# A fused decoder layer on one core: attention outputs issued for four steps at a time, with six buffers of turned probabilities and an earlier copy of one pattern's turned values

## What is computed

```python
ATTN_PATTERNS = ((128, 1), (512, 4), (2048, 16))      # window, dilation; 8 slots of 64 in each
scores = jnp.einsum("brnqhd,brnkhd->brnhqk", qb, kb) * (ATTN_HEAD_DIM ** -0.5)
scores = jnp.where(valid[None, None, :, None], scores, -jnp.inf)
m = jnp.max(scores, axis=-1, keepdims=True)
p = jnp.exp(scores - m)
den = jnp.sum(p, axis=-1)
o = jnp.einsum("brnhqk,brnkhd->brnqhd", p, vb) / jnp.moveaxis(den, -1, -2)[..., None]
lse = jnp.moveaxis(m[..., 0] + jnp.log(den), -1, -2)
```

## Time and profile before

| | |
|---|---|
| median of three runs | 2852.78 us (2850.05 to 2854.59) |
| the profiled execution | 2852.36 us, of which the span of its instructions is 2850.7 us |
| TensorE's mean granted clock | 0.987 |
| TensorE busy | 2760.1 us (97% of the span) |
| VectorE, ScalarE, GpSimd busy | 55%, 43%, 55% |
| attention block | from about 1975 to 2281 us |
| matmuls of the scores in it (L1658) | 768 |
| transposes of probabilities (L1669) | 600 |
| output products (L87 into a_pso) | 2400 |

### The profile page before, as it was taken

The page is one execution under the profiler, slowest core; times in us unless marked ns, Lnnn a source line. Parts: engine busy times, 40 slices in busy tenths (PEclk is TensorE's granted clock), DMA queues, the critical chain, the costliest instruction groups (busy, mean ns, idle before and its releaser), DMA issues. The chain is left out here.

```text
span 2850.7 us, 44158 instructions
## 1 busy us (share of the span) xinstructions
PE 2760.1 (97%) x15998; PEld 2295.0 (81%) x15998; DVE 1581.4 (55%) x2527; ACT 1238.0 (43%) x2258; POOL 1576.6 (55%) x1078
## 2 busy tenths in 40 slices
PE   6999999999999999999998999999999889999998
PEld 5888888888887888888887788887988777778787
DVE  6335334897544346885424555555777686743433
ACT  5232234333224533332234565565777654532332
POOL 7677778877777788777773454553111254322000
PEclk8999999999999999999999999999999999999999
DMA  3556345433225345332135454555665478855543
GB/s 125 142 171 216 132 133 154 129 117 96 69 72 192 118 150 148 112 110 74 60 119 185 150 187 149 191 171 168 188 204 177 126 247 257 297 186 171 170 148 110
DMA packets 462813, 436.24 MB, mean 153 GB/s; under 512 B 60736, under 2 KB 403008, under 8 KB 454976
## 3 DMA queue, kind: packets, MB, share of 16 engines
q1 hardware_dynamic: 460352, 425.79, 47.7%
q0 software_dynamic: 2304, 8.39, 0.8%
HBM read 290.99 MB, written 143.13 MB: 152 GB/s over the span
## 5 line engine op out<-in xcount | busy, mean ns | idle before, releaser
L550 PE MATMUL p_acc<-h_kept,w_hi 128*128 128x512 f32 x1216 | 475.4, 391 | 4.6 <-ACT work L596 3.1
L552 PE MATMUL p_acc<-h_kept,w_lo 128*128 128x512 f32 x1216 | 474.1, 390 | 0.0
L551 PE MATMUL p_acc<-h_kept,w_hi 128*128 128x512 f32 x1216 | 474.1, 390 | 0.0
L431 POOL TENSOR_TENSOR w_lo<-p_sums,w_hi 128x512 fp32r<-128x512 f32 x300 | 390.8, 1319 | 131.4 <-ACT w_hi L637 131.4
L637 ACT ACTIVATE w_hi<-p_sums 128x512 fp32r<-128x512 f32 x300 | 189.0, 632 | 471.8 <-PE p_acc L552 449.0
L550 PEld LDWEIGHTS p_acc<-h_kept,w_hi 128*128 128x128 f32 x1216 | 228.8, 188 | 53.9 <-ACT work L596 3.3
L552 PEld LDWEIGHTS p_acc<-h_kept,w_lo 128*128 128x128 f32 x1216 | 228.8, 188 | 47.6
L551 PEld LDWEIGHTS p_acc<-h_kept,w_hi 128*128 128x128 f32 x1216 | 228.9, 188 | 47.1
L550 PE MATMUL p_acc<-p_ops,w_hi 128*128 128x512 f32 x608 | 238.0, 391 | 7.1 <-DVE p_ops L738 7.1
L551 PE MATMUL p_acc<-p_ops,w_hi 128*128 128x512 f32 x608 | 237.3, 390 | 0.0
L552 PE MATMUL p_acc<-p_ops,w_lo 128*128 128x512 f32 x608 | 237.1, 390 | 0.0
(11 more groups left out here) (344 smaller groups left out, 6725.2 us busy)
## 6 DMA issues: line engine op xcount, KB each, us to landing
raw<-w_in SPq DMA_DIRECT2D x100, 512.0 KB, 4.7
s_qs<-p_stage SPq DMA_DIRECT2D x96, 256.0 KB, 3.9
work<-s_gates SPq DMA_DIRECT2D x48, 512.0 KB, 7.3
p_rawb<-w_in SPq DMA_DIRECT2D x38, 512.0 KB, 3.7
keep<-w_in SPq DMA_DIRECT2D x38, 512.0 KB, 4.8
s_xbc<-p_stage SPq DMA_DIRECT2D x32, 512.0 KB, 2.6
work<-s_xbc SPq DMA_DIRECT2D x16, 1024.0 KB, 6.4
spare<-s_qs SPq DMA_DIRECT2D x16, 1024.0 KB, 5.7
```

What stands on the lines that cost most here:

```text
L431: tt(w_lo[:, k], weight(u, k), w_hi[:, k], ALU.subtract).then_inc(w_made, 1)
L550: pe.matmul(bank, hi, ops[k][:, 0, c], start=c == 0, stop=False)
L551: pe.matmul(bank, hi, ops[k][:, 1, c], start=False, stop=False)
L552: last = pe.matmul(bank, lo, ops[k][:, 0, c], start=False, stop=c == 3)
```

## The change

TensorE does the outputs of four steps in every fourth step instead of those of two in every second; the turned probabilities get six buffers instead of four; VectorE copies the two groups of such a visit in the second and the third step after it instead of one in each even step; and the copies of pattern two's turned values wait for output 48i - 9, the last that reads the old ones, instead of output 48i - 4.

```diff
-        probs_t = s.sb("a_probst", [P, 4, 4, P])
+        probs_t = s.sb("a_probst", [P, 6, 4, P])
...
         def evacuate(eng, parity, copy, j):
 
             eng.wait_ge(p_turned, j + 5)
-            eng.wait_ge(o_made, j + 1)
+            eng.wait_ge(o_made, max(j - 1, 1))
...
-                copy(probs_t[:, j % 4], ps_t[:, n % 4]).then_inc(t_taken[parity], 1)
+                copy(probs_t[:, j % 6], ps_t[:, n % 4]).then_inc(t_taken[parity], 1)
...
             if pair:
-                eng.wait_ge(o_made, NS * (pair - (g == 0)) + {0: 4 * SPAN + 4, 1: 1, 2: 4}[g])
+                eng.wait_ge(o_made, NS * (pair - (g == 0)) + {0: 4 * SPAN + 4, 1: -4, 2: 4}[g])
...
-                    if j >= 4 and j % 2:
-                        output(j - 5)
-                        output(j - 4)
+                    if j >= 4 and j % 4 == 3:
+                        for n in range(j - 7, j - 3):
+                            output(n)
...
-                for j in range(ALL + 5):
+                for j in range(ALL + 7):
...
-                    if j >= 6 and j % 2 == 0:
-                        grp = j // 2 - 3
+                    if j >= 9 and j % 4 in (1, 2):
+                        grp = (j - 9) // 4 * 2 + (j % 4 == 2)
```

More of the change, by code:

```diff
@@ L1481, in evacuate @@
             if width(g, b) == width(g, b + 1) == 2 * P:
-                copy(probs_t[:, j % 4], ps_t[:, n % 4]).then_inc(t_taken[parity], 1)
+                copy(probs_t[:, j % 6], ps_t[:, n % 4]).then_inc(t_taken[parity], 1)
             elif width(g, b + 1) == P:
-                copy(probs_t[:, j % 4, 1::2], ps_t[:, n % 4, 1::2]).then_inc(t_taken[parity], 1)
+                copy(probs_t[:, j % 6, 1::2], ps_t[:, n % 4, 1::2]).then_inc(t_taken[parity], 1)
             else:
-                copy(probs_t[:, j % 4, 1:], ps_t[:, n % 4, 1:]).then_inc(t_taken[parity], 1)
+                copy(probs_t[:, j % 6, 1:], ps_t[:, n % 4, 1:]).then_inc(t_taken[parity], 1)
         def evacuate_v(eng, parity, copy, which):
@@ L1685, in output @@
                         for h in range(first, 2):
-                            last = matmul_by_columns(pe, ps_o[:, j // 2 % 2, (b + e) % 4, :OUT_W], probs_t[:, j % 4, 2 * e + h],
+                            last = matmul_by_columns(pe, ps_o[:, j // 2 % 2, (b + e) % 4, :OUT_W], probs_t[:, j % 6, 2 * e + h],
                                                      v_tok[:, g, b + e - 1 + h, sl * OUT_W:(sl + 1) * OUT_W],
```

## The result

The changed kernel takes 2861.86 us (median of 20 runs), the kernel before 2853.48 us (20 runs beside it); the ratio is 1.0029, with a 95% interval of 1.0021 to 1.0038. It is slower, by 8.4 us where 7.5 were forecast. The profiled execution took 2861.93 us, 9.6 more than that of before.

What follows compares the result with a forecast made beforehand. TensorE was taken to set the attention stage's pace. Terms -16.1 - 3.4 + 11.7 + 5.0 + 7.2 + 1.5 + 1.6 gave +7.5, so 2860.4 us, range 2850 to 2868.

Steps and rivals of the forecast that it cites:

- visits, 46 x 0.35: TensorE going to the outputs and back costs 0.35 us; 46 fewer visits up to step 188: 16.1 us less.
- waits that go: Pattern two's value copy (3 x 0.8) and transposes waiting in steps 84 to 87 (3 x 0.35): 3.4 us less.
- new waits, 18 wide stretches: Without a visit between, transposes wait for exponentials in four-step wide stretches: 0.65 us each, 11.7 us more.
- new waits, 15 narrow ones: Pattern three's stretches with narrow pieces: 0.33 us each, the middle between 0 and 0.7, 5.0 us more.
- keys, longer waits of TensorE: Second head's key load, queued behind pattern three's store, comes later; wait grows 2.4 in each of three pairs: 7.2 us.
- lower clock behind them: TensorE's clock falls behind the first pair's key wait too: 1.6 us more, between 0 and 4.8.
- tail: Copy of group 91 moves from step 188 to 190, delaying SyncE's queue at the attention stage's end: 1.5 us more.
- The walk: Step-by-step timing of a wide four-step stretch: transposes late by 0.22 and 0.35, with restarts 0.7 us together.
- Only the visits count: Rival: bursts don't wait, the chain being short enough or queues far enough ahead; 2843.7 us, chance 0.12.
- Keys in time: Rival: the key load lands earlier, so neither the 7.2 nor the clock is paid; 2851.6 us, chance 0.12.
- A lower clock in the bursts: Rival: the clock falls in a third of the 18 wide stretches, 9.6 us more; 2870 us, chance 0.06.
- The earlier copy brings nothing: Rival: another wait ends last at pattern two's values, so 2.4 us more; 2862.8 us, chance 0.05.

Runs made afterwards that it cites:

- run 3: Kernel before with one step's outputs in every step, so twice as many visits: ratio 1.0047 to the kernel before.
- run 8: Kernel before with six buffers of turned probabilities alone: ratio 0.9998 to the kernel before.
- run 7: Kernel before with only pattern two's turned values copied on their last reader: 2849.52 us, ratio 0.9984.
- runs 1 and 2: Keys of head two loaded before pattern two's store, in the changed kernel (0.9969, 2844.8 us) and in the kernel before (0.9963, 2843.78 us).
- run 9: Changed kernel with the next block's loads before the store of pattern two in the last pair: ratio 1.0005 to the kernel before.
- run 6: Changed kernel with early keys, transposes three steps after the scores and visits one step later: ratio 1.0006 to the kernel before.
- run 4: Changed kernel with each group of outputs copied one step earlier: ratio 1.0055 to the kernel before.
- run 5: Changed kernel with transposes three steps after the scores instead of two, turned-tile copies moved along: ratio 1.0054 to the kernel before.

## Why the prediction was right, step by step

From the first score to that of step 188 the changed kernel takes 8.92 us more; the stretches, each difference with 0.35 us for the visit that it no longer has, split that up. What TensorE waited behind the key splits, and what the clock took there, are worked out below.

| step of the prediction | forecast | measured |
|---|---|---|
| visits, 46 x 0.35 | -16.1 | -16.1 by a price of 0.35: 0.35 in run 3, 0.34 in steps 8 to 11 of the changed kernel |
| waits that go | -3.4 | about -2.9 |
| new waits, 18 wide stretches | +11.7 | +11.9 |
| new waits, 15 narrow ones | +5.0 | +5.2 |
| keys, longer waits of TensorE | +7.2 | +7.5 |
| lower clock behind them | +1.6 | +3.0 |
| steps 0 to 3 of pair zero, without a visit | 0 | +0.3 |
| tail | +1.5 | +1.9 |

The measured terms add up to the 10.85 us by which the block grew, 3.35 more than the forecast. The profiled executions are 9.6 apart, as the first score came 2.2 earlier and what follows the block took 1.0 longer; the medians are 8.4 apart, with an interval of the ratio that reaches from 6.0 to 10.8 us. So the mechanism and the signs were right and most terms too, but that the time came within 1 us of the forecast is partly luck.

The walk gave a loss of 0.22, 0.35 and two restarts of 0.06 in a wide stretch, and 0.26, 0.32 and the same restarts came. The middle value taken for narrow stretches was a guess between two bounds, and that it fell so well is luck: 0.27 and 0.42 in the two halves of pattern three, 0.35 on average.

*Waits that go.* The 0.8 us for the copy of pattern two's values was 0.61, in the changed kernel and alone (run 7). The sum for steps 96 to 99 left out small gaps behind value transposes. The 0.35 of steps 84 to 87 came as forecast, but neither by the six buffers (run 8) nor by the earlier values (run 7): it takes the new order of visits, and why is not shown.

*Keys.* TensorE's three waits behind the key splits were 1.56 and 2.03 and 2.24 us, and are 4.50, 4.41 and 4.41:

```profile
2222.55 0.66 PE L1669 MATMUL a_pst<-ident,a_probs 128*128 128x128 f32 x4 [2.24 <-ACT a_probs L1720]
```

```profile
2073.97 1.12 PE L1669 MATMUL a_pst<-ident,a_probs 128*128 128x128 f32 x4 [4.50 <-ACT a_probs L1720]
...
2150.99 1.12 PE L1669 MATMUL a_pst<-ident,a_probs 128*128 128x128 f32 x4 [4.41 <-ACT a_probs L1720]
...
2227.23 1.12 PE L1669 MATMUL a_pst<-ident,a_probs 128*128 128x128 f32 x4 [4.41 <-ACT a_probs L1720]
```

They grew by 2.9, 2.4 and 2.2, together 7.5 where 3 x 2.4 were forecast. At the second of them the copy, SyncE's issue of the keys right behind the store, and the split are:

```profile
2135.53 0.42 DVE L1776 COPY att_all<-a_pso 128x260 f32<-128x260 f32 x1
```

```profile
2136.59 3.44 SPq L977 DMA_DIRECT2D work<-s_kv  x2
```

```profile
2147.86 1.91 ACT L1507 ACTIVATE key_hi<-work 128x2048 fp32r<-128x2048 f32 x1 [5.02 <-DMA work<-s_kv]
```

With step 96 at 2124.70, the copy came at 10.8 (10.7 forecast, 9.5 before), and the keys 12.3 behind it (12.2 before). ScalarE stood ready at 18.1, where it was 19.8, so its own wait grew by 3.05. TensorE's grew by less, 2.4, as forecast. What the late loads cost is shown by runs 1 and 2.

*Clock.* This term was too small: 1.6 forecast, 3.0 measured, as what the waits leave of the 10.5 us in the three stretches. The windows of 6 us from the end of each wait say the same. Before, the granted clock is 1.00 behind the first, and behind the second (and, with the same 0.72, the third)

```profile
2147.23:2153.23 6.00, 6.00 (x76) 5.36 (x76) 2.23 (x10) 3.99 (x10) 6.00 (x4) 0.72 0.24 67
```

and in the changed kernel

```profile
2073.97:2079.97 6.00, 6.00 (x67) 5.67 (x69) 2.23 (x10) 4.59 (x11) 6.00 (x4) 0.59 0.26 81
2150.99:2156.99 6.00, 6.00 (x79) 5.76 (x80) 2.14 (x10) 4.59 (x11) 6.00 (x4) 0.75 0.33 101
2227.23:2233.23 6.00, 6.00 (x61) 5.67 (x63) 2.23 (x10) 4.58 (x11) 3.40 (x1) 0.56 0.21 60
```

By these windows 0.28 x 6 us are lost twice before, 3.4 in all, and now 0.41, 0.25 and 0.44 x 6 us, 6.6 in all: 3.2 more. The prediction counted one more fall, in pair one, at the size of the old ones; the falls in pairs one and three are also longer. It reads a mean clock of 0.60 as half of the time at the lower level, too: between 1.00 and 0.50 a mean of 0.60 is four fifths of the time. The 1.6 us are not touched by that.

*Tail.* One more step than before to the copy and the queue behind it; run 9 shows the queue, and that 6 us could be taken out of it.

*The rule on PSUM.* By amount VectorE and ScalarE had time to spare, and I let the walk decide against that. The Trainium skill (TensorEngine Tiling (Array Packing), Performance Considerations) says that the copies out of PSUM may become the bottleneck. The runs show a middle course: VectorE's masks and copies, which all read PSUM, do limit TensorE, but in the burst alone, where they are 1.2 us a step against 0.92 (run 6), and by the order in which they come (run 4).

*The rivals.* Only the visits count: out, the waits are there. Keys in time: out, they came later still. A lower clock in the bursts: no, between the key waits it is 1.00 (2080 to 2150 and 2155 to 2225 us of the changed kernel), with the waits of 0.3 us in it. The earlier copy brings nothing: in the changed kernel it brought 0.61 three times, but what it brings before the key split is lost there, as run 7 shows.

## What to carry to other kernels

A cost of switching between two kinds of work is saved by doing each in longer runs, but a longer run of one kind asks the engines behind it for its pace, not for the average: write down the first four steps of the burst with the durations of the trace, buffer by buffer, before counting the switches. Then look for what hangs on the step at which something is handed over, a store and behind it in the same queue a load: here three loads behind a store turned a change that is worth nothing by itself into a loss, and moving them shortened their stretches by 9 us in the old kernel and by 18 in the new one. And a gain ahead of a wait for a DMA is no gain until the DMA moves as well.

## What was not expected of the hardware

- The stages before the attention are the same code in all fourteen profiled executions, and yet the first score starts between 1974.3 and 1993.5 us; what follows the attention block takes 568.4 to 572.3 us. The block itself repeats to a hundredth of a microsecond in most stretches. So a difference of 2 us in the block is plain in the trace and can hardly be seen in the times.
- The length of a wait alone doesn't tell whether TensorE's clock falls behind it. Behind waits of 1.56 (before) and 1.66 us (run 8) it stayed at full speed, behind 1.79 (run 8), 1.93 (run 7), 2.03 and 2.24 us (before) it fell, each time to a mean of 0.72 over the 6 us behind the wait. But in run 6 it fell behind two waits of 1.78 us and not behind two others of the same length, and in run 5 a wait of 1.85 us in front of an output (at 2117.93) left it at 1.00. What decides it is open. The price is plain: 1.55 us for a fall in run 6, and for 0.37 us more of waiting run 7 pays 1.9 in the stretch. Falls differ in length: with waits of 4.50, 4.41 and 4.41 us the changed kernel's key stretches take 12.40, 11.43 and 12.45.
- A second launch of work on an engine can start before the one ahead has ended: VectorE's mask began 0.34 us after a copy of 0.42 us. Sums over busy time are too long by that; starts, not lengths, give the pace.
